# Chunk matmuls of a two-block model: evacuations wait on the count of used chunks instead of a count of finished groups

## What is computed

```python
for l in range(DEPTH):                                   # DEPTH = 2
    x = x + 0.5 * swiglu(rms_norm(x, ffn1_norm[l]), ...)
    proj = rms_norm(x, mix_norm[l]) @ w_in[l]            # 1024 -> 3328
    mixed = concat(rwkv7_group(proj[..., :1792]), retnet_group(proj[..., 1792:]))
    x = x + mixed @ w_out[l]
    x = x + 0.5 * swiglu(rms_norm(x, ffn2_norm[l]), ...)
return rms_norm(x, final_norm)
```

## Time and profile before

| | |
|---|---|
| median of 3 runs | 2420.69 us |
| lowest, highest | 2415.8, 2423.4 us |
| the profiled execution | 2423.87 us |
| its span, first to last instruction | 2421.7 us |
| mean granted clock of TensorE | 0.985 |
| VectorE busy | 1418.9 us (59%) |
| ScalarE busy | 982.4 us (41%) |
| DMA | 458.02 MB, mean 189 GB/s |

### The profile page before, as it was taken

How to read it: one execution, slowest core, us unless ns; L and a number is a source line. 1 busy time by engine, 2 the same in 40 slices (tenths; PEclk the granted TensorE clock), 3 DMA queues, 4 the chain that set the end, 5 groups by cost and what they waited for, 6 DMA issues and landing times.

```text
span 2421.7 us, 37290 instructions
## 1 busy us (share of the span) xinstructions
PE 2294.5 (95%) x13918; PEld 1878.9 (78%) x13918; DVE 1418.9 (59%) x1893; ACT 982.4 (41%) x1245; POOL 101.6 (4%) x82
## 2 busy tenths in 40 slices
PE   9999999999999999999999898999999889999997
PEld 7998888899899888889988576866666677666664
DVE  5666767666666567666664356633348565533377
ACT  5554522444555453244443234332237333322264
POOL 0000023000000003200000000000000000000000
PEclk9999999999999999999999999999999999999998
DMA  6667501566566761046656242489989441599985
GB/s 194 187 187 218 169 10 35 170 186 182 158 182 185 222 192 44 1 145 186 187 178 189 91 157 91 148 287 338 331 297 335 163 157 61 193 340 342 316 307 205
DMA packets 386961, 458.02 MB, mean 189 GB/s; under 512 B 18542, under 2 KB 273170, under 8 KB 386706
## 3 DMA queue, kind: packets, MB, share of 16 engines
q1 hardware_dynamic: 381824, 446.35, 57.5%
q10 hardware_dynamic: 5010, 9.98, 1.3%
HBM read 451.56 MB, written 1.05 MB: 187 GB/s over the span
## 4 chain that ended last, share of the span: by engine, by line
PE 49%; issue 37%; DVE 7%; DMA 2%; POOL 2%; ACT 2%; SPq 1%; ACTq 0%; DVEq 0%; POOLq 0%; PEldq 0%
PE PS L2306 4%; PE PS L2114 4%; PE PS L2116 3%; PE PS L2115 3%; PE PS L2310 2%; PE PS L2392 2%; PE PS L2133 2%; PE PS L2394 2%; PE PS L2393 2%; PE PS L2134 2%; PE PS L2135 2%; PE PS L2243 2%; PE PS L2245 1%; PE PS L2244 1%; PE PS L2686 1%
## 5 line engine op out<-in xcount | busy, mean ns | idle before, releaser
L1312 DVE TENSOR_TENSOR wlo<-raw,whi 128x1024 fp32r<-128x1024 f32 x336 | 410.2, 1224 | 446.6 <-ACT whi L828 443.6
L828 ACT ACTIVATE whi<-raw 128x1024 fp32r<-128x1024 f32 x336 | 354.2, 1057 | 501.0 <-PE PS L2116 379.0
L2114 PE MATMUL PS<-xTh,whi 128*128 128x256 f32 x1792 | 512.8, 286 | 5.6 <-DVE xTl L1279 4.0
L2115 PE MATMUL PS<-xTl,whi 128*128 128x256 f32 x1792 | 506.8, 283 | 0.0
L2116 PE MATMUL PS<-xTh,wlo 128*128 128x256 f32 x1792 | 506.7, 283 | 0.0
L2114 PEld LDWEIGHTS PS<-xTh,whi 128*128 128x128 f32 x1792 | 343.0, 191 | 41.8 <-issue 32.7
L2115 PEld LDWEIGHTS PS<-xTl,whi 128*128 128x128 f32 x1792 | 343.2, 192 | 3.2
L2116 PEld LDWEIGHTS PS<-xTh,wlo 128*128 128x128 f32 x1792 | 343.2, 191 | 0.0
L2392 PE MATMUL PS<-whi,xTh 128*128 128x416 f32 (+2 forms) x480 | 181.9, 379 | 18.5 <-DVE xTl L1279 7.5
L2133 PE MATMUL PS<-whi,hTh 128*128 128x512 f32 x448 | 179.0, 400 | 4.3 <-DVE wlo L1312 4.3
L2394 PE MATMUL PS<-whi,xTl 128*128 128x416 f32 (+2 forms) x480 | 177.3, 369 | 0.0
(11 more groups left out here) (516 smaller groups left out, 3875.2 us busy)
## 6 DMA issues: line engine op xcount, KB each, us to landing
raw<-in_ffn_w_gate_dram SPq DMA_DIRECT2D x88, 512.0 KB, 5.3
raw<-in_ffn_w_up_dram SPq DMA_DIRECT2D x88, 512.0 KB, 6.3
raw<-in_ffn_w_down_dram SPq DMA_DIRECT2D x88, 512.0 KB, 3.7
raw<-in_l_e_gate_dram SPq DMA_DIRECT2D x64, 512.0 KB, 6.0
raw<-in_l_e_up_dram SPq DMA_DIRECT2D x64, 512.0 KB, 6.4
raw<-in_l_e_down_dram SPq DMA_DIRECT2D x64, 512.0 KB, 5.6
ring<-in_l_e_up_dram SPq DMA_DIRECT2D x64, 512.0 KB, 6.5
ring<-in_l_e_gate_dram SPq DMA_DIRECT2D x64, 512.0 KB, 6.7
```

The source lines that it names most:

```text
L828: nc.scalar.activation(whi[:, m if slot is None else slot], raw[:, m, j], ACT.Copy).then_inc(hi_done[m], 1)
L1312: nc.vector.tensor_tensor(wlo[:, w], raw[:, m, j], whi[:, w].bitcast(F32), ALU.subtract).then_inc(lo_done[m], 1)
L2114: mm(out_, whi[:, m, ks], xTh[:, k, :], start=(k == 0), stop=False)
L2115: mm(out_, whi[:, m, ks], xTl[:, k, :], start=False, stop=False)
```

## The change

The counter `group_done` is deleted. TensorE no longer waits for its own last matmul at the end of a group, and no longer increments anything there; only the pool matmuls keep their wait, for `xT_psum`. Those who waited for n + 3 groups now wait for the count of used chunks that the last matmul of that group produces. `group_used(n)` gives this count in the second block; the groups 40 and 41 share one set of four chunks, hence the case at `POOL_GROUPS_AT`.

```diff
+POOL_GROUPS_AT = 40
...
-        group_done = sem("group_done")
...
+        def group_used(n):
+
+            return 4 * (n if n < POOL_GROUPS_AT else n - 1) + 4 + 4
...
                 def evac_in(n):
-                    act.wait_ge(group_done, 10 * l + n + 1 + CR)
+                    act.wait_ge(chunk_used, 40 * l + 4 * n + 4 + 4)
...
             def evac(n, dst, rooted=False):
-                act.wait_ge(group_done, n + 1 + CR)
+                act.wait_ge(chunk_used, group_used(n))
...
             def evac_turned(n, dst, j):
-                act.wait_ge(group_done, n + 1 + CR)
+                act.wait_ge(chunk_used, group_used(n))
...
-                    dve.wait_ge(group_done, 10 * l + 8 + j + 1 + CR)
+                    dve.wait_ge(chunk_used, 40 * l + 32 + 6 + 2 * j + 4)
                     xs = x[:, :, j * 512:(j + 1) * 512]
...
-                dve.wait_ge(group_done, n + 1 + CR)
+                dve.wait_ge(chunk_used, group_used(n))
...
-                        dve.wait_ge(group_done, n + 2 + CR)
+                        dve.wait_ge(chunk_used, group_used(n + 1))
...
-            pe.sem_inc(group_done, CR)
...
-            def group_end(n4):
-
-                pe.wait_ge(chunk_used, 4 * n4 + 4 + 4)
-                pe.sem_inc(group_done, 1)
-
...
-                group_end(n4)
...
-                    if i == 5 or i == 7:
-                        pe.wait_ge(chunk_used, 40 * l + 32 + i + 1 + 4)
-                        pe.sem_inc(group_done, 1)
...
                         pe.wait_ge(chunk_used, 4 * n4 + 2 * j + 2 + 4)
-                        pe.sem_inc(group_done, 1)
                         pe.sem_inc(xT_psum, 2)
```

## The result

| | before | after |
|---|---|---|
| median of the runs | 2418.39 us (6 runs, 2414.61 to 2423.4) | 2398.06 us (6 runs, 2393.0 to 2408.72) |
| ratio after / before | | 0.9925, interval 0.9907 to 0.9943 |
| profiled execution | 2423.87 us, span 2421.7 | 2393.0 us, span 2390.8 |
| mean granted clock of it | 0.985 | 0.990 |

By the ratio the change makes the kernel faster by about 18 us (14 to 22); the two medians lie 20.3 apart. A second set of six runs gave 2402.96 (ratio 0.9935, 0.9915 to 0.9954), which is just inside it.

A forecast was written before the change was run, and what follows sets the result against it. TensorE, busy 95% of the span, was taken as the bound, so time is won only where it stands still or other engines' chains shorten. First block 6.0 plus second 5.8 gave 11.8 us, from 2420.69 to 2409.0, range 2402.5 to 2417.5.

The forecast's parts named there:

- The price of a border: At group ends, TensorE's wait for its own last matmul costs 0.65 (mixer), 0.54 (512 wide, turned), 0.46 us (memory groups).
- Mixer input: Borders of the eight mixer input groups, each layer: 2.5 us gained, part of the offer lost to late splits.
- Mixer output: Two halves of the mixer output, each layer: 0.4 us at the first, 0.1 at the second, sum 0.5.
- the eighth input border: Last mixer input border: about 0.1 us, because ScalarE's evacuation sees the matmul's own count and saves the counter step.
- step through the counter: Evacuating engines that see the matmul's own count save one step of TensorE's queue, 0.1 us, counted only on the path.
- Second block: 28 borders of the second block: 5.8 us gained in sum, with 12 of the borders yielding nothing.
- The trap in the residual pairs: Eight borders of four residual pairs yield nothing: VectorE's chain holds the third chunk, whose stall grows from 0.3 to about 0.85.
- Added: nothing: ScalarE and VectorE wait for the same event under another name; cost between -0.1 us and 0.
- The mixer output ends about 3 us earlier in layer 1: Sign in the trace after: mixer output ends about 3 us earlier in the first layer, about 6 after the second.
- The first block at equal clock: Mixer input and output of both layers in the first block: 2 x 3.0 = 6.0 us gained.
- The base: Starting time from which the gain of 11.8 us was subtracted: 2420.69 us, the median of the runs.
- rival C: Whole kernel: more time at half clock cancels the gain from 23 us, slower from about 38, 2428 to 2432; chance 0.05.

The follow-up runs named there:

- the experiment at equal clock: `free_second`: kernel after, with wait and increment kept in the first block, only the second block's borders free; 2414.03 us, 0.9975 of before.
- pe_both: Kernel after, with TensorE's wait and increment back at all 48 borders, evacuating engines still reading the count of used chunks; 2419.16 us, 1.0004 of before.
- keep_wait: Kernel after, with TensorE's wait for its own last matmul kept at 46 borders, second counter and increments gone; 2409.34 us, 0.9964 of before.
- b_extra: Kernel before, with 16 more TensorE waits for its own last matmul, behind the second chunk of each mixer input group; 2423.24 us, 1.0019 of before.

## Why the prediction was wrong, point by point

- *The price of a border* (0.65, 0.54, 0.46): right as a sum. It consists of 0.49 for the wait and 0.16 for the increment behind it in the mixer, of 0.33 and 0.21 at 512 wide in the second block.
- *Mixer input* 2.4 of the 2.5 a layer: 2.2 measured. The fourth chunks of groups 2 and 4 have VectorE as releaser, as said.
- *Mixer output* 0.5: 0.25 inside it. Around it the eighth input border and the second layer's end gave 0.4 and 0.25, where I had 0.1 for each. At the eighth border I had counted only the evacuation's step through the counter and not the stop itself, which ahead of the transposes is 0.66 - 0.19 = 0.47 (298.85 - 298.19 in before). Both layers: 6.2 against 6.0.
- *Second block* 5.8: 6.3 by the stretches, 5.9 by the experiment at equal clock.
- *The trap in the residual pairs*: right, the stall of 0.85 too, and shown from both sides.
- *Added: nothing*: right; `pe_both` shows it for the evacuating engines. It also shows that the 0.1 which I counted for a step through the counter can't be seen in the total (1.0004, with 2416.0 against 2416.4 at equal clock).
- *"The mixer output ends about 3 us earlier in layer 1"*: wrong as an observation, it ends 10.4 earlier. 3.2 of this is the late weight DMA and its half clock ahead of the first group, 4.5 the drop behind the eighth.
- *The first block at equal clock* is 8.0, not 6.0. The stretches that I can compare without a drop give 6.2; the feed-forward stage between the layers scatters by 2 us in profiles without a drop (402 to 404), so I can't say whether anything is gained there.
- *The base*: I subtracted from 2420.69, the median of three runs. That of the 115 later ones is 2418.7, so 2.0 of the 10.9 us between forecast and result are the base.
- **The step that failed** is rival C and what I made of it for the range. I took the clock as a risk of losing (0.05), and as noise of 2 to 5 us with mean zero; a gain by it had no term in the sum. Measured: +0.0022 of mean clock, 4.8 us, beside 13.3 at equal clock. So the 10.9 us are 2.0 of the base, 1.5 of the borders (13.3 for 11.8), 4.8 of the clock, and 2.6 of luck: the first six runs had a mean clock of 0.9890, the second six 0.9872, and the mean of all twelve is 2400.7. Without the 4.8 that mean would lie inside the range. Why the clock rises stays open. The rival even names the rule of the Trainium skill that speaks for a gain (TensorE: Matmul & The Clock Gate, What's actually happening: the clock follows how busy TensorE has been), and gave it no microsecond. As a measure of the amount the runs don't bear it out: `keep_wait` has 0.9880 with all waits, and `b_extra` with 16 more has 0.9869. In the trace of before nine stretches at half clock add up to 73 us; at the 4.5 us that 10.2 of them cost, some 32 us were at stake, nearly three times the whole sum. The range should have reached 5 to 8 us further down.
- The same page of the Trainium skill, in the same section, says that the amount of slow matmuls varies from one run of a kernel to the next, since what watches the activity does not start anew with a kernel. The traces agree: same instructions on TensorE, drop in both layers of before, in none of `pe_both`.

## What to carry to other kernels

In this kernel a wait of TensorE for its own last matmul costs 0.33 to 0.49 us where nothing else is late, plus 0.16 to 0.21 for an increment queued behind it, and a consumer can as well wait for the matmuls' own count. But look at who is late next: eight of the borders here gave nothing until VectorE's order was changed as well. And when two profiles are compared, first add up the time at the lower clock in each, and compare stretches without it; a difference of 31 us held 13 that the change's own waits explain.

## What the runs showed of the hardware

- The time at half clock is a matter of the single execution: before alone had mean clocks from 0.982 to 0.990 and times from 2407.8 to 2430.2, at 2.2 us for each 0.001.
- Spare matmuls in two waits of 1.2 and 0.6 us, ahead of a place where the clock often dropped, raised the mean clock from 0.9859 to 0.9894, worth 7 us.
- More idle time does not always mean a lower clock: 16 added stops of up to half a microsecond left it at 0.9869, and 46 waits kept without their increments had 0.9880, where before has 0.9859. What sets it is open.
- An increment in TensorE's queue is free behind a running stream (2403.4 against 2403.1 for 46 of them) and costs 0.16 to 0.21 us behind a wait.
